# Narrow matmul passes of a decode-and-prefill kernel: gate columns joined to wide units, the compressed branch issued between them, and scores for head pairs

## The chip, the cores and the metric

One core of one Trainium2 chip runs the whole program in one launch. The metric is the device time of that launch in microseconds, lower is better; the shown time is a median of three runs.

## The reference

Two layers are computed for 512 prompt tokens and for 8 sequences of 8 new tokens each (D = 1024, all in 32-bit floats). Layer A is a matrix-memory layer with a pooled branch; layer C is sparse attention with three branches: compressed keys and values, selected pages, and a sliding window. What the change touches is the projection of layer C and the prompt's compressed branch:

```python
q, kc_raw, vc_raw, ks, vs, kw, vw, gate_logits(48), z = split(rmsnorm(x) * mod @ c_w_in)
gates   = sigmoid(gate_logits + b_gate)                  # 16 heads x 3 branches
pooled  = sum over blocks of 32 tokens (stride 16) of pos * raw        # 31 blocks for the prompt
kc, vc  = gelu(pooled @ w1 + b1) @ w2                    # keys get a rotary position
out     = gates[0]*attend(q, kc, vc) + gates[1]*selected + gates[2]*window
y       = x + gate * ((out * silu(z)) @ c_w_out)
```

## The kernel before

The program is a row of blocks, each with a stream of its own for TensorE (PE), VectorE (DVE), ScalarE (ACT), GpSimd (POOL) and SyncE (SP), tied by semaphores. All engines meet in a barrier between two blocks. The order of work within a stream is written out by hand.

The **projection of layer C** is `project(pe, "c", plan_c, ...)`. `plan_c` is a list of units, and a unit is one output tile: kind "T" (token-major, at most 128 tokens x 512 columns; the 128x128 activations are the stationary weights, the weight matrix moves), kind "F" (feature-major, 128 features x 576 tokens in two halves of 288), kind "N" (narrow). Before, they were: units 0 to 4 "T" for the raw compressed keys and values (`W_CC`), 5 to 8 "F", 9 to 13 "T", 14 to 21 "F" for the queries, 22 to 29 "F" for z, and 30 to 34 "N", the 48 gate columns for five tiles of tokens. Each unit sums over KT = 8 slices of D. Units rotate over three pairs of PSUM banks (0 to 5), ACT copies each out (L1229 for T, L1236 and L1237 for F, L1231 for N), and PE starts unit u only after unit u-3 was copied. Banks 6 and 7 are for the rotary position: one unit behind each key or query unit, `swap` issues two matmuls (L1209, L1210), and DVE does four operations (L1283 to L1289). Tiles 0 to 3 of a "T" or "N" group have 128 prompt tokens each, tile 4 the samples' 64.

After the projection, DVE adds the gate bias (L1300) and ACT takes the sigmoid (L1240). A **second block** computes the prompt's compressed branch: pooling matmuls (L1350), the gate rows of the samples (L1354), the hidden layer (L1310, then ACT L1314), the keys in two forms (L1318, L1319), the values (L1364), and DVE's part of it, which ends with the gate rows (L1391, L1394). A **third block** is the attention. It begins with `prompt_cmp_scores` for both halves of the heads (L1528), which DVE masks (L1633) and takes a maximum of (L1639), while PE goes on to `pe_pool` (L1679, L1686). SP and POOL send the cached pages from this block's start (L1520).

A 32-bit matmul shows in the trace as two passes, each a LDWEIGHTS and a MATMUL record, so that a unit of 8 matmuls is 16 passes.

Of the kernel before, what the change touches and what calls it, by code (L numbers as in the profile page):

```python
# [17 lines left out]
P = 128  # L18
# [3 lines left out]
NB = 8  # L22
# [231 lines left out]
def build(nc, v):  # L254

    with ExitStack() as ctx:
# [48 lines left out]
        plan_c += [(W_ZC + n // 4, "F", n) for n in range(8)] + [(None, "N", n) for n in range(5)]  # L305
# [26 lines left out]
        def project(pe, name, plan, moving, narrow, between=None, ready=None, each_step=None, halves_apart=None):  # L332
# [16 lines left out]
            for i, (chunk, kind, index) in enumerate(plan):  # L349
# [39 lines left out]
                elif kind == "T":  # L389
                    m = P if index < 4 else NS  # L390
                    for k in range(KT):
                        last = pe.matmul(main[0:m, :], moving[k][:, index * P:index * P + m], w[:, k, :],  # L392
                                         start=(k == 0), stop=(k == KT - 1))
                        if k == 2:
                            add_parts()
                elif name == "a":
                    for k in range(KT):
                        pe.matmul(main[0:H, :], narrow[:, k, H * index:H * index + H], moving[k][:, 0:TP],
                                  start=(k == 0), stop=(k == KT - 1))
                        if k == 2:  # L400
                            add_parts()
                    for k in range(KT):
                        last = pe.matmul(samp[0:H, 0:NS], narrow[:, k, H * index:H * index + H], moving[k][:, TP:NT],
                                         start=(k == 0), stop=(k == KT - 1))
                else:
                    m = P if index < 4 else NS
                    for k in range(KT):
                        last = pe.matmul(main[0:m, 0:48], moving[k][:, index * P:index * P + m], narrow[:, k, 8:56],
                                         start=(k == 0), stop=(k == KT - 1))
# [657 lines left out]
        kcP = take(2 * NC_P).rearrange("p (c n) -> p c n", c=2)  # L1067
# [93 lines left out]

        in_d, swapped, roped, set_up = sem("in_d"), sem("swapped"), sem("roped"), sem("set_up")
# [5 lines left out]
        with nc.Block() as block:  # L1168
            @block.sync
            def _(sp):  # L1170
                sp.dma_start(constD, v["constD"]).then_inc(in_d, 16)
                sp.dma_start(constC, v["constC"]).then_inc(in_d, 16)
                sp.dma_start(ktmp_[:, 0:320], v["pool_masks"]).then_inc(in_d, 16)
                sp.dma_start(narrow_, v["narrow"]).then_inc(in_d, 16)
# [12 lines left out]
            def _(pool):  # L1187
                pool.memset(gates_, 0.0)
                pool.memset(qblk, 0.0)
                pool.memset(w1b, 0.0)  # L1190
# [3 lines left out]
            def _(pe):  # L1194
                def ready(i):
                    if i < 4:
                        pe.wait_ge(nC.h_prompt, i + 1)
                    if i == 4:
                        pe.wait_ge(nC.h_sample, 1)
                    if i == 5:  # L1200
                        pe.wait_ge(in_d, 64)
# [10 lines left out]
                project(pe, "c", plan_c, [hC[:, k, :] for k in range(KT)], narrow, between=swap, ready=lambda i, _: ready(i))  # L1212

            @block.scalar
            def _(act):
# [7 lines left out]
                for i, (chunk, kind, index) in enumerate(plan_c):  # L1223
# [6 lines left out]
                    elif chunk is None:  # L1230
                        last = act.activation(gates[0:m, index, :], main[0:m, 0:48], ACT.Copy)  # L1231
# [7 lines left out]
                act.wait_ge(gate_sum, 1)  # L1239
                act.activation(gates_, gates_, ACT.Sigmoid).then_inc(gate_sig, 1)  # L1240

            @block.vector
            def _(dve):
# [17 lines left out]
                dve.wait_ge(in_d, 64)  # L1261
# [12 lines left out]
                for g in range(2):  # L1274
                    rows, o = slice(g * DH, g * DH + DH), g * DH
                    dve.tensor_copy(w2b[rows, 2, o:o + 8], sm("w2k")[rows, 8:16])
                    dve.tensor_copy(w2b[rows, 2, o + 8:o + 16], sm("w2k")[rows, 0:8])
                for n in range(12):
# [20 lines left out]
                dve.wait_ge(proj_evac, u0c + len(plan_c))  # L1299
                dve.tensor_tensor(gates, gates, sm("b_gate").unsqueeze(1).to_broadcast([P, 5, 48]), ALU.add).then_inc(gate_sum, 1)  # L1300
# [4 lines left out]

        def compress_dve_pool(dve, n):
            return dve.tensor_tensor(pooled[:, :, 0:n], lohi[:, :, 0, 0:n], lohi[:, :, 1, 1:n + 1], ALU.add)
# [21 lines left out]

        def compress_dve_keys(dve, kcT, n, bank, bank2):  # L1330
            cos = cd("cmp_cos")[:, 0:n].unsqueeze(1).to_broadcast([P, 2, n])
            sin = cd("cmp_sin")[:, 0:n].unsqueeze(1).to_broadcast([P, 2, n])
            a = ps[:, bank, 0:2 * n].rearrange("p (c n) -> p c n", c=2)
            b = ps[:, bank2, 0:2 * n].rearrange("p (c n) -> p c n", c=2)
            dve.tensor_tensor(kcT[:, :, 0:n], a, cos, ALU.mult)
            dve.tensor_tensor(ktmp[:, :, 0:n], b, sin, ALU.mult)
            dve.drain()
            return dve.tensor_tensor(kcT[:, :, 0:n], kcT[:, :, 0:n], ktmp[:, :, 0:n], ALU.add)

        pe_p, act_p, dve_p = sem("pe_pcmp"), sem("act_pcmp"), sem("dve_pcmp")  # L1340
        PE2 = Order(["pool", "gates", "hidk", "hidv", "kc", "vc"])
        AC2 = Order(["hk", "hv", "vcs"])
        DV2 = Order(["lohi", "pooled", "kcT", "gates"])
        with nc.Block() as block:
            @block.tensor
            def _(pe):
                for c in range(4):
                    for t in range(4):
                        out = ps[:, 0, c * P:(c + 1) * P].rearrange("p (l n) -> p l n", l=2)[:, :, t * 8:t * 8 + 8]
                        last = pe.matmul(out, ccz[:, t, c * P:c * P + P], wpos[:, c // 2], start=True, stop=True)  # L1350
                last.then_inc(pe_p, PE2.one("pool"))
                rt = cc_("row_token", NS).rearrange("p (b n) -> p b n", b=NB)
                for b in range(NB):
                    last = pe.matmul(ps[:, 2, b * 48:b * 48 + 48], rt[:, b, :], gates[0:NS, 4, :], start=True, stop=True)  # L1354
                last.then_inc(pe_p, PE2.one("gates"))
                pe.wait_ge(dve_p, DV2["pooled"])
                compress_pe_hidden(pe, 0, NC_P, 1).then_inc(pe_p, PE2.one("hidk"))
                compress_pe_hidden(pe, 1, NC_P, 7).then_inc(pe_p, PE2.one("hidv"))
                pe.wait_ge(act_p, AC2["hv"])
                compress_pe_keys(pe, NC_P, 3, 4).then_inc(pe_p, PE2.one("kc"))  # L1360
                for gp in range(2):
                    for g2 in range(2):
                        rows = slice(g2 * DH, g2 * DH + DH)
                        last = pe.matmul(ps[g2 * NC_P:g2 * NC_P + NC_P, 5, gp * DH:gp * DH + DH], hid[rows, 2 + gp, 0:NC_P],  # L1364
                                         sm("w2v")[rows, :], start=True, stop=True)
                last.then_inc(pe_p, PE2.one("vc"))

            @block.scalar
            def _(act):
                act.wait_ge(pe_p, PE2["hidk"])  # L1370
                compress_act_hidden(act, 0, NC_P, 1).then_inc(act_p, AC2.one("hk"))
                act.wait_ge(pe_p, PE2["hidv"])
                compress_act_hidden(act, 1, NC_P, 7).then_inc(act_p, AC2.one("hv"))
                act.wait_ge(pe_p, PE2["vc"])
                act.activation(vcP, ps[0:2 * NC_P, 5, 0:P], ACT.Copy).then_inc(act_p, AC2.one("vcs"))

            @block.vector
            def _(dve):
                dve.memset(lohi[:, :, 1, NC_P:NC_P + 1], 0.0)
                dve.wait_ge(pe_p, PE2["pool"])  # L1380
                dve.tensor_copy(lohi[:, :, :, 0:32], ps[:, 0, :].rearrange("p (c l n) -> p c l n", c=4, l=2)[:, :, :, 0:32])\
                    .then_inc(dve_p, DV2.one("lohi"))
                dve.drain()
                compress_dve_pool(dve, NC_P).then_inc(dve_p, DV2.one("pooled"))
                dve.wait_ge(pe_p, PE2["kc"])
                compress_dve_keys(dve, kcP, NC_P, 3, 4).then_inc(dve_p, DV2.one("kcT"))
                dve.wait_ge(pe_p, PE2["gates"])
                dve.drain()
                g3_ = ktmp.rearrange("p c n -> p (c n)")[:, 0:NB * 48]
                g3 = g3_.rearrange("p (b c) -> p b c", b=NB)  # L1390
                dve.tensor_tensor(g3, ps[:, 2, 0:NB * 48].rearrange("p (b c) -> p b c", b=NB),  # L1391
                                  cc_("row_head").unsqueeze(1).to_broadcast([P, NB, 48]), ALU.mult)
                dve.drain()
                dve.tensor_reduce(grow, g3_.rearrange("p (b h c) -> p b c h", b=NB, c=3), AX.X, ALU.add)\  # L1394
                    .then_inc(dve_p, DV2.one("gates"))

# [126 lines left out]
        def prompt_cmp_scores(pe, gp):  # L1523
            for r in range(R):
                for t in range(4):
                    for g2 in range(2):
# [914 lines left out]
```

## Time and profile before

| | |
|---|---|
| median of three runs | 1384.14 us (1380.78 to 1392.83) |
| the profiled execution | 1385.89 us, span 1384.2 us |
| mean granted TensorE clock | 0.930 |
| PE busy | 1244.8 us, 90% |
| PEld (weight loads) busy | 782.9 us, 57% |
| DVE, ACT, POOL busy | 485.4, 412.9, 175.3 us |

The units 0 to 34 of the projection stand from 511.26 to 764.5 us, the second block from 766.7 to 782.2 us, and the attention from 782.3 us to the end. "idle before <- releaser" behind a row says how long the engine had been idle and who ended it. A granted clock of 1.00 is 2.4 GHz and 0.50 is 1.2 GHz.

### The profile page before, as it was taken

The page shows a single profiled execution, that of the slowest core. Times are in us where ns is not written, and L with a number is a line of the kernel's source. Part 1 is how long each engine was busy: PE and PEld are TensorE (multiplying, and loading weights), DVE is VectorE, ACT ScalarE, POOL GpSimd, SP SyncE. Part 2 cuts the span into 40 slices and gives each one's busy share as a digit, 9 for nine tenths or more (in the row PEclk, how much of TensorE's full clock was granted, in tenths as well). Part 3 has the DMA queues.
Part 4 walks back from the last instruction along what each step waited for, and adds up shares of the span by engine and source line. Part 5 has one row for each costly group of instructions (what it writes and reads, how often), then busy time and mean ns, then how long its engine had stood idle before and what let it go on. Part 6 is the DMA issues. An engine that isn't in the chain of part 4 may idle for free. (4 is left out here: it accounts for less than half of the span.)

```text
span 1384.2 us, 25565 instructions
## 1 busy us (share of the span) xinstructions
PE 1244.8 (90%) x9287; PEld 782.9 (57%) x9287; DVE 485.4 (35%) x1478; ACT 412.9 (30%) x1088; POOL 175.3 (13%) x287
## 2 busy tenths in 40 slices
PE   4899999992986979999999889999999799989996
PEld 1676755751654744747778845555555434444455
DVE  2352120004564240101210175556555433333334
ACT  3311111112220031000101146565556433333443
POOL 0000000001000000000000122222222353343300
PEclk8999999995786989999999589999999999999998
DMA  9414333338003131212300377666666698999972
GB/s 388 171 61 182 122 122 122 122 133 280 24 10 121 61 135 36 74 38 75 125 0 1 110 262 241 223 224 230 224 229 222 231 342 296 329 318 318 339 268 70
DMA packets 94905, 238.01 MB, mean 172 GB/s; under 512 B 11450, under 2 KB 49468, under 8 KB 90300
## 3 DMA queue, kind: packets, MB, share of 16 engines
q1 hardware_dynamic: 74076, 169.26, 35.0%
q0 software_dynamic: 20704, 67.13, 13.5%
q8 instruction: 74, 1.21, 0.4%
q14 instruction: 51, 0.42, 0.1%
HBM read 227.68 MB, written 17.05 MB: 177 GB/s over the span
## 5 line engine op out<-in xcount | busy, mean ns | idle before, releaser
L385 PE MATMUL ps<-arena,wring 128*128 128x288 f32 x1664 | 416.9, 412 | 6.9 <-DMA wring<-in_weights 5.4
L385 PEld LDWEIGHTS ps<-arena,wring 128*128 128x128 f32 x1664 | 318.2, 192 | 100.0 <-issue 8.0
L1520 POOL DMA_DIRECT2D arena<-in_cmp_pages x128 | 70.1, 549 | 489.5 <-issue 278.7
L392 PE MATMUL ps<-wring,arena 128*128 128x512 f32 (+1 forms) x240 | 107.8, 608 | 7.1 <-ACT arena L1220 7.1
L1614 DVE CUSTOM_DVE_ANT_0 wring<-ps,wring 128x128 f32<-128x128 f32 (+3 forms) x128 | 57.6, 488 | 75.8 <-PE ps L1543 74.1
L392 PEld LDWEIGHTS ps<-wring,arena 128*128 128x128 f32 (+1 forms) x240 | 43.4, 184 | 67.5 <-issue 60.3
L1606 ACT ACTIVATE wring<-ps 128x128 f32<-128x128 f32 (+3 forms) x128 | 49.0, 436 | 90.8 <-PE ps L1566 90.8
L2079 DVE CUSTOM_DVE_ANT_1 arena<-ps,small 128x512 f32<-128x512 f32 x64 | 44.3, 693 | 89.7 <-PE ps L1998 89.6
L2055 ACT ACTIVATE arena<-arena 128x512 f32<-128x512 f32 (+1 forms) x88 | 57.0, 649 | 60.1 <-DVE arena L2095 60.1
L1592 ACT ACTIVATE wring<-wring 128x128 f32<-128x128 f32 (+3 forms) x128 | 70.7, 559 | 8.4 <-DVE wring L1614 8.3
L1679 PE MATMUL ps<-arena 128*32 128x256 f32 x1024 | 70.1, 391 | 0.0
L2066 ACT ACTIVATE arena<-ps 128x512 f32<-128x512 f32 x72 | 43.0, 597 | 84.9 <-PE ps L2019 84.9
L1283 DVE SCALAR_TENSOR_TENSOR arena<-ps,arena 128x512 f32<-128x512 f32 x12 | 8.3, 693 | 151.7 <-PE ps L1210 151.7
L2141 PE MATMUL ps<-arena 128*128 128x512 f32 x128 | 60.8, 630 | 0.0
L1543 PE MATMUL ps<-arena 64*128 64x512 f32 (+3 forms) x256 | 52.9, 490 | 5.4 <-DVE wring L1614 5.4
L1962 POOL DMA_DIRECT2D wring<-in_kv_pages x64 | 45.2, 711 | 80.6 <-PE ps L2033 39.2
L1236 ACT ACTIVATE arena<-ps 128x288 f32<-128x288 f32 x20 | 8.2, 412 | 151.6 <-PE ps L385 151.6
L2019 PEld LDWEIGHTS ps<-fixed,arena 128*128 128x128 f32 x288 | 30.8, 140 | 39.4 <-ACT arena L2055 24.4
L1998 PE MATMUL ps<-wring,arena 128*64 128x512 f32 x144 | 39.5, 629 | 10.6 <-DMA wring<-in_win_kv 7.1
L1583 PE MATMUL ps<-wring,arena 128*64 128x128 f32 x640 | 48.7, 282 | 0.0
L1566 PE MATMUL ps<-fixed,wring 128*128 128x128 f32 x320 | 47.8, 280 | 1.1 <-ACT wring L1606 1.1
L1998 PE MATMUL ps<-arena 128*64 128x512 f32 x144 | 41.1, 655 | 7.7 <-DMA arena<-in_win_kv 7.4
(383 smaller groups left out, 1572.7 us busy)
## 6 DMA issues: line engine op xcount, KB each, us to landing
wring<-in_weights SPq DMA_DIRECT2D x27, 2048.0 KB, 9.0
arena<-in_cmp_pages SPq DMA_DIRECT2D x128, 256.0 KB, 3.5
arena<-in_cmp_pages POOLq DMA_DIRECT2D x128, 256.0 KB, 4.3
wring<-in_kv_pages SPq DMA_DIRECT2D x64, 256.0 KB, 9.3
wring<-in_kv_pages POOLq DMA_DIRECT2D x64, 256.0 KB, 6.8
arena<-in_kv_pages SPq DMA_DIRECT2D x50, 256.0 KB, 6.5
arena<-in_kv_pages POOLq DMA_DIRECT2D x50, 256.0 KB, 6.9
arena<-in_out_tiles SPq DMA_DIRECT2D x12, 512.0 KB, 8.4
```

The source lines that it names most:

```text
L385: last = pe.matmul(out[:, 0:HT], w[:, k, ct * P:ct * P + P], moving[k][:, half * HT:half * HT + HT], start=(k == 0), stop=(k == KT - 1))
L392: last = pe.matmul(main[0:m, :], moving[k][:, index * P:index * P + m], w[:, k, :], start=(k == 0), stop=(k == KT - 1))
L1520: eng.dma_start(cring[q % CR][:, 2 * half + j, :], v["cmp_pages"][bass.ds(ids[2 * d + j], 1)] .rearrange("o p c -> (o p) c")).then_inc(c_i ...
L1543: last = pe.matmul(ps[:, SB + g2, 0:(t + 1) * P], qT[rows, u, t * P:t * P + P], kk[rows, 2 * br + u // 4, 0:(t + 1) * P], start=True, stop ...
L1583: last = pe.matmul(ps[g2 * DH:g2 * DH + DH, OB, t * P:t * P + P], vv[:, n, o:o + DH], PTb[:, tile_no[i] % 3, g2, n * P:n * P + P], start=F ...
L1592: act.activation(Pb[:, b, h, 0:s], Pb[:, b, h, 0:s], ACT.Exp, scale=-1.0, bias=negm[:, b, h:h + 1], accum_out=sums[:, b, h:h + 1]).then_in ...
L1606: act.activation(PTb[:, tile_no[i] % 3, h, 0:s], ps[:, TB + h, 0:s], ACT.Copy).then_inc(act_a, AC3.one(("e", i, h)))
L1614: dve.tensor_tensor_reduce(Pb[:, b, h, 0:(t + 1) * P], ps[:, SB + h, 0:(t + 1) * P], causal4[:, (3 - t) * P:TP], -1.0, 3.0e38, ALU.add, AL ...
L1679: last = pe.matmul(ps[32 * j:32 * j + 32, half, x * KVW:x * KVW + KVW], wpool[:, x, 32 * q:32 * q + 32], page[:, j, x * KVW:x * KVW + KVW] ...
L1998: last = pe.matmul(out, qblk[:, gp, n, gp * DH:gp * DH + DH], keys, start=True, stop=True)
L2055: last = act.activation(SS[:, o:o + w], SS[:, o:o + w], ACT.Exp, scale=sign, bias=negmax[:, which:which + 1], accum_out=sums11[:, n % 2, c ...
L2141: last = pe.matmul(ps[:, 0, :], tile_w[:, k, :], zT[:, k, 0:TP], start=(k == 0), stop=(k == KT - 1))
```

## The change

1. The five "N" units of layer C go. Each of the units 0 to 4 gets, behind each of its 8 wide matmuls, a narrow one with the same stationary activations and the 48 gate columns, into the pair's other bank. ACT copies 48 more columns in each of these units. The narrow weights are sent first by SP, under a semaphore of their own, and DVE adds the gate bias ahead of the rotary work; ACT takes the sigmoid after unit 13.
2. The second block goes. Its matmuls are issued by `prompt_compressed` after the units 23 (`AT_POOL`: pooling and gate rows), 25 (`AT_HIDDEN`) and 27 (`AT_KEYS`: keys and values), in banks 6 and 7. ACT's gelu stands behind the copies of unit 25, its copy of the values behind unit 29. DVE's part stands behind the rotary work and `qblk`.
3. The compressed keys `kcP` become block diagonal over the two heads of a pair, with zeros from a POOL memset, so that one matmul with 128 contraction rows and 64 moving columns gives the scores of both heads, where before two matmuls with 64 rows and 32 columns each did. DVE's mask is four operations a half, of 256 elements a row, where it was two of 512.

```diff
-        plan_c += [(W_ZC + n // 4, "F", n) for n in range(8)] + [(None, "N", n) for n in range(5)]
+        plan_c += [(W_ZC + n // 4, "F", n) for n in range(8)]
...
                         last = pe.matmul(main[0:m, :], moving[k][:, index * P:index * P + m], w[:, k, :],
                                          start=(k == 0), stop=(k == KT - 1))
+                        if chunk == W_CC:
+                            last = pe.matmul(samp[0:m, 0:48], moving[k][:, index * P:index * P + m], narrow[:, k, 8:56],
+                                             start=(k == 0), stop=(k == KT - 1))
...
-        kcP = take(2 * NC_P).rearrange("p (c n) -> p c n", c=2)
+        kcP = take(4 * NC_P).rearrange("p (c n) -> p c n", c=2)
...
+        AT_POOL, AT_HIDDEN, AT_KEYS = 23, 25, 27
...
+                sp.dma_start(narrow_, v["narrow"]).then_inc(in_narrow, 16)
                 sp.dma_start(constD, v["constD"]).then_inc(in_d, 16)
...
+                def prompt_compressed(i):
+                    if i == AT_POOL:
+                        pe.wait_ge(roped, 12)
+                        for c in range(4):
+                            for t in range(4):
+                                out = ps[:, 6, c * P:(c + 1) * P].rearrange("p (l n) -> p l n", l=2)[:, :, t * 8:t * 8 + 8]
+                                last = pe.matmul(out, ccz[:, t, c * P:c * P + P], wpos[:, c // 2], start=True, stop=True)
+                        last.then_inc(pe_p, PE2.one("pool"))
+                        pe.wait_ge(gate_sig, 1)
+                        rt = cc_("row_token", NS).rearrange("p (b n) -> p b n", b=NB)
+                        for b in range(NB):
+                            last = pe.matmul(ps[:, 7, b * 48:b * 48 + 48], rt[:, b, :], gates[0:NS, 4, :], start=True, stop=True)
+                        last.then_inc(pe_p, PE2.one("gates"))
+                    if i == AT_HIDDEN:
+                        pe.wait_ge(dve_p, DV2["pooled"])
...
+                    if i == AT_KEYS:
+                        pe.wait_ge(act_p, AC2["hv"])
+                        pe.wait_ge(dve_p, DV2["gates"])
...
+                def after_unit(i):
+                    swap(i)
+                    prompt_compressed(i)
...
-                    for g2 in range(2):
-                        rows, o = slice(g2 * DH, g2 * DH + DH), (r * 4 + t) * NC_P
-                        last = pe.matmul(ps[:, SB + 2 * gp + g2, o:o + NC_P], qT[rows, gp * 4 + r, t * P:t * P + P],
-                                         kcP[rows, gp, 0:NC_P], start=True, stop=True)
+                    o = (r % 2 * 4 + t) * 2 * NC_P
+                    last = pe.matmul(ps[:, SB + 2 * gp + r // 2, o:o + 2 * NC_P], qT[:, gp * 4 + r, t * P:t * P + P], kcP[:, gp, :],
+                                     start=True, stop=True)
```

On PE, at the start of layer C's projection (units 0 to 4, then unit 5 and 6), stood before:

```order
L392 MATMUL ps<-wring,arena 128x512 x32
L392 MATMUL ps<-wring,arena 64x512 x8
L385 MATMUL ps<-arena,wring 128x288 x32
L1209 MATMUL ps<-arena 128x512
L1210 MATMUL ps<-arena 128x64
```

Now the same place reads as follows, where "..." stands for 31 more such pairs, and after it for 7 more:

```order
L392 MATMUL ps<-wring,arena 128x512
L395 MATMUL ps<-arena 128x48
...
L392 MATMUL ps<-wring,arena 64x512
L395 MATMUL ps<-arena 64x48
...
L385 MATMUL ps<-arena,wring 128x288 x32
L1221 MATMUL ps<-arena 128x512
L1222 MATMUL ps<-arena 128x64
```

Behind each of the 40 wide matmuls, which stood in a row, there is now a narrow one.

On PE, from the last rotary swap (behind unit 22) to the first scores and `pe_pool`, stood before (L1168 and L1344 are the ends of the first and the second block):

```order
L1209 MATMUL ps<-arena 128x512
L1210 MATMUL ps<-arena 128x64
L385 MATMUL ps<-arena,wring 128x288 x112
L408 MATMUL ps<-arena 128x48 x32
L408 MATMUL ps<-arena 64x48 x8
L1168 UNCONDITIONAL_BRANCH
L1345 UNCONDITIONAL_BRANCH
L1350 MATMUL ps<-arena 128x2x8 x16
L1354 MATMUL ps<-arena 128x48 x8
...
L1528 MATMUL ps<-arena 128x32 x64
```

Now there stands (L1177 is the end of the only block left there):

```order
L385 MATMUL ps<-arena,wring 128x288 x16
L1230 MATMUL ps<-arena 128x2x8 x16
L1235 MATMUL ps<-arena 128x48 x8
L385 MATMUL ps<-arena,wring 128x288 x32
L1240 MATMUL ps<-arena 128x64 x2
L385 MATMUL ps<-arena,wring 128x288 x32
L1246 MATMUL ps<-arena 128x64 x2
L1252 MATMUL ps<-small,arena 32x64 x4
L385 MATMUL ps<-arena,wring 128x288 x32
L1177 UNCONDITIONAL_BRANCH
L2210 UNCONDITIONAL_BRANCH
L1532 MATMUL ps<-arena 128x64 x32
```

The row of 112 wide matmuls (units 23 to 29) is cut in four, the narrow groups stand in the cuts, and the scores are 32 matmuls where they were 64.

## Rows read from the trace of the kernel before

**Rows 1.** Waits, 510 to 800 us: who waited for whom, total, times, longest.
```profile
DVE arena L1283 <- PE ps L1210: 151.7, 12, 45.0
```

**Rows 2.** Timeline of PE at the end of the projection: start us, us, instructions.
```profile
752.33 12.18 PE L408 MATMUL ps<-arena 128*128 128x48 f32 x80
766.77 6.98 PE L1350 MATMUL ps<-arena 128*128 128x16 f32 x32 [2.27 <-PEq L1168]
773.68 3.65 PE L1354 MATMUL ps<-arena 64*128 64x48 f32 x16
777.26 1.11 PE L1310 MATMUL ps<-arena 128*128 128x64 f32 x4
...
779.82 0.64 PE L1364 MATMUL ps<-small,arena 64*32 64x64 f32 x8
782.30 13.86 PE L1528 MATMUL ps<-arena 64*128 64x32 f32 x128 [1.84 <-PEq L1344]
796.09 1.93 PE L1679 MATMUL ps<-arena 128*32 128x256 f32 x16
```

**Rows 3.** Stretches: us, busy time by engine, PEclk, DMA share, GB/s.
```profile
516.00:520.00 4.00, 4.00 (x9) 1.65 (x9) 3.79 (x16) 4.00 (x11) 0.00 (x0) 0.86 0.00 0
752.00:756.00 4.00, 4.00 (x37) 3.89 (x35) 0.00 (x0) 0.93 (x3) 0.00 (x0) 1.00 0.02 4
756.00:760.00 4.00, 4.00 (x21) 4.00 (x20) 0.00 (x0) 0.42 (x2) 0.00 (x0) 0.51 0.00 0
...
790.00:796.00 6.00, 6.00 (x58) 6.00 (x58) 0.74 (x2) 0.00 (x0) 0.79 (x2) 0.50 1.03 386
796.00:800.00 4.00, 4.00 (x32) 1.73 (x33) 3.56 (x5) 0.00 (x0) 0.00 (x0) 0.50 0.49 179
```

**Rows 4.** Timeline of ACT at the end of the projection.
```profile
752.83 0.41 ACT L1237 ACTIVATE arena<-ps 128x288 f32<-128x288 f32 x1
754.24 0.21 ACT L1231 ACTIVATE arena<-ps 128x48 f32<-128x48 f32 x1 [1.00 <-PE ps L408]
756.03 0.21 ACT L1231 ACTIVATE arena<-ps 128x48 f32<-128x48 f32 x1 [1.57 <-PE ps L408]
759.26 0.21 ACT L1231 ACTIVATE arena<-ps 128x48 f32<-128x48 f32 x1 [3.01 <-PE ps L408]
762.67 0.21 ACT L1231 ACTIVATE arena<-ps 128x48 f32<-128x48 f32 x1 [3.20 <-PE ps L408]
764.54 0.20 ACT L1231 ACTIVATE arena<-ps 64x48 f32<-64x48 f32 x1 [1.66 <-PE ps L408]
...
766.06 0.41 ACT L1240 ACTIVATE arena<-arena 128x240 f32<-128x240 f32 x1
...
780.51 0.27 ACT L1375 ACTIVATE arena<-ps 64x128 f32<-64x128 f32 x1 [1.78 <-PE ps L1364]
```

**Rows 5.** Timeline of PE around the last rotary swap.
```profile
688.90 8.00 PE L385 MATMUL ps<-arena,wring 128*128 128x288 f32 x32
...
697.60 0.33 PE L1210 MATMUL ps<-arena 128*128 128x64 f32 x2
697.77 54.72 PE L385 MATMUL ps<-arena,wring 128*128 128x288 f32 x224
```

**Rows 6.** Timelines of PE and of ACT at the start of the projection.
```profile
511.26 37.65 PE L392 MATMUL ps<-wring,arena 128*128 128x512 f32 x80 [7.07 <-ACT arena L1220]
...
528.20 0.60 ACT L1229 ACTIVATE arena<-ps 128x512 f32<-128x512 f32 x1 [6.20 <-PE ps L392]
535.07 0.60 ACT L1229 ACTIVATE arena<-ps 128x512 f32<-128x512 f32 x1 [6.27 <-PE ps L392]
```

**Rows 7.** Timeline of DVE: its last copies, the gate rows, a half's mask.
```profile
700.66 2.16 DVE L1297 COPY arena<-arena 64x64 f32<-64x64 f32 x16
...
781.31 0.67 DVE L1394 TENSOR_REDUCE arena<-arena 128x24 f32<-128x384 f32 x1
...
796.20 1.29 DVE L1633 TENSOR_TENSOR wring<-ps,wring 128x512 f32<-128x512 f32 x2 [5.46 <-PE ps L1528]
```

More of the change, by code:

```diff
@@ L403, in project @@
                         last = pe.matmul(samp[0:H, 0:NS], narrow[:, k, H * index:H * index + H], moving[k][:, TP:NT],
[L404 to L408, printed above, removed]
                                          start=(k == 0), stop=(k == KT - 1))
@@ L1197, in ready @@
                         pe.wait_ge(nC.h_prompt, i + 1)
+                    if i == 0:
+                        pe.wait_ge(in_narrow, 16)
                     if i == 4:
@@ L1210, in swap @@
                         pe.matmul(ps[:, 7, 0:NS], cc_("swap"), rope_tile[n][:, TP:NT], start=True, stop=True).then_inc(swapped, 1)
-                project(pe, "c", plan_c, [hC[:, k, :] for k in range(KT)], narrow, between=swap, ready=lambda i, _: ready(i))
+                def prompt_compressed(i):
[13 more added lines that the diff above has]
+                        pe.wait_ge(dve_p, DV2["pooled"])
+                        for x, name in enumerate(("hidk", "hidv")):
+                            pe.matmul(ps[:, 6, 2 * x * NC_P:2 * x * NC_P + 2 * NC_P].rearrange("p (c n) -> p c n", c=2), w1b[:, x, :],
+                                      pooledP[:, 2 * x:2 * x + 2], start=True, stop=True).then_inc(pe_p, PE2.one(name))
+                    if i == AT_KEYS:
+                        pe.wait_ge(act_p, AC2["hv"])
+                        pe.wait_ge(dve_p, DV2["gates"])
+                        for x, weights in enumerate((w2b[:, 0, :], w2b[:, 2, :])):
+                            last = pe.matmul(ps[:, 7, 2 * x * NC_P:2 * x * NC_P + 2 * NC_P].rearrange("p (c n) -> p c n", c=2), weights,
+                                             hidP[:, 0:2], start=True, stop=True)
+                        last.then_inc(pe_p, PE2.one("kc"))
+                        for g2 in range(2):
+                            rows, outs_ = slice(g2 * DH, g2 * DH + DH), slice(g2 * NC_P, g2 * NC_P + NC_P)
+                            for gp in range(2):
+                                last = pe.matmul(ps[outs_, 6, gp * DH:gp * DH + DH], hidP[rows, 2 + gp], sm("w2v")[rows, :],
+                                                 start=True, stop=True)
+                        last.then_inc(pe_p, PE2.one("vc"))
@@ L1214, in _ @@
+                def after_unit(i):
+                    swap(i)
+                    prompt_compressed(i)
+                project(pe, "c", plan_c, [hC[:, k, :] for k in range(KT)], narrow, between=after_unit, ready=lambda i, _: ready(i))
             @block.scalar
@@ L1229, in _ @@
                         last = act.activation(out[0:m, :], main[0:m, :], ACT.Copy)
-                    elif chunk is None:
-                        last = act.activation(gates[0:m, index, :], main[0:m, 0:48], ACT.Copy)
+                        if chunk == W_CC:
+                            last = act.activation(gates[0:m, index, :], samp[0:m, 0:48], ACT.Copy)
                     else:
@@ L1238, in _ @@
                     last.then_inc(proj_evac, 1)
-                act.wait_ge(gate_sum, 1)
-                act.activation(gates_, gates_, ACT.Sigmoid).then_inc(gate_sig, 1)
+                    if i == 13:
+                        act.wait_ge(gate_sum, 1)
+                        act.activation(gates_, gates_, ACT.Sigmoid).then_inc(gate_sig, 1)
+                    if i == AT_HIDDEN:
+                        for x, name in enumerate(("hk", "hv")):
+                            act.wait_ge(pe_p, PE2["hidv"])
+                            act.activation(hidP[:, 2 * x:2 * x + 2], ps[:, 6, 2 * x * NC_P:2 * x * NC_P + 2 * NC_P].rearrange("p (c n) -> p c n", c=2),
+                                           ACT.Gelu_apprx_tanh, bias=sm("b1kv"[:2] + "kv"[x])[:, 0:1]).then_inc(act_p, AC2.one(name))
+                act.wait_ge(pe_p, PE2["vc"])
+                act.activation(vcP, ps[0:2 * NC_P, 6, 0:P], ACT.Copy).then_inc(act_p, AC2.one("vcs"))
             @block.vector
@@ L1277, in _ @@
                     dve.tensor_copy(w2b[rows, 2, o + 8:o + 16], sm("w2k")[rows, 0:8])
+                dve.wait_ge(proj_evac, u0c + 5)
+                dve.tensor_tensor(gates, gates, sm("b_gate").unsqueeze(1).to_broadcast([P, 5, 48]), ALU.add).then_inc(gate_sum, 1)
                 for n in range(12):
@@ L1298, in _ @@
                                             qT[rows, gp * 4 + r, TP:NT].rearrange("p (b t) -> p b t", b=NB))
[L1299 to L1307, printed above, removed]
+                dve.wait_ge(pe_p, PE2["pool"])
+                dve.memset(lohiP[:, :, 1, NC_P:NC_P + 1], 0.0)
+                dve.tensor_copy(lohiP[:, :, :, 0:NC_P], ps[:, 6, :].rearrange("p (c l n) -> p c l n", c=4, l=2)[:, :, :, 0:NC_P])\
+                    .then_inc(dve_p, DV2.one("lohi"))
+                dve.drain()
+                dve.tensor_tensor(pooledP, lohiP[:, :, 0, 0:NC_P], lohiP[:, :, 1, 1:NC_P + 1], ALU.add).then_inc(dve_p, DV2.one("pooled"))
+                dve.wait_ge(pe_p, PE2["gates"])
+                g3 = gates3_.rearrange("p (b c) -> p b c", b=NB)
+                dve.tensor_tensor(g3, ps[:, 7, 0:NB * 48].rearrange("p (b c) -> p b c", b=NB),
+                                  cc_("row_head").unsqueeze(1).to_broadcast([P, NB, 48]), ALU.mult)
+                dve.drain()
+                dve.tensor_reduce(grow, gates3_.rearrange("p (b h c) -> p b c h", b=NB, c=3), AX.X, ALU.add)\
+                    .then_inc(dve_p, DV2.one("gates"))
+                dve.wait_ge(pe_p, PE2["kc"])
+                cos = cd("cmp_cos")[:, 0:NC_P].unsqueeze(1).to_broadcast([P, 2, NC_P])
+                sin = cd("cmp_sin")[:, 0:NC_P].unsqueeze(1).to_broadcast([P, 2, NC_P])
+                dve.drain()
+                dve.tensor_tensor(ktmpP[:, 0:2], ps[:, 7, 0:2 * NC_P].rearrange("p (c n) -> p c n", c=2), cos, ALU.mult)
+                dve.tensor_tensor(ktmpP[:, 2:4], ps[:, 7, 2 * NC_P:4 * NC_P].rearrange("p (c n) -> p c n", c=2), sin, ALU.mult)
+                dve.drain()
+                for g2 in range(2):
+                    rows = slice(g2 * DH, g2 * DH + DH)
+                    last = dve.tensor_tensor(kcP[rows, :, g2 * NC_P:g2 * NC_P + NC_P], ktmpP[rows, 0:2], ktmpP[rows, 2:4], ALU.add)
+                last.then_inc(dve_p, DV2.one("kcT"))
         def compress_pe_hidden(pe, x, n, bank):
@@ L1340, in build @@
[L1340 to L1361, printed above, removed]
-                    for g2 in range(2):
[L1363 to L1395, printed above, removed]
@@ L1630, in prompt_cmp_mask @@
             dve.wait_ge(pe_a, PE3["sc%d" % gp])
-            add = pcmp_add.rearrange("p (t n) -> p t n", t=4).unsqueeze(1).to_broadcast([P, R, 4, NC_P])
-            for g2 in range(2):
-                last = dve.tensor_tensor(pc[:, gp, g2::2, :].rearrange("p (r t) n -> p r t n", r=R),
-                                         ps[:, SB + 2 * gp + g2, :].rearrange("p (r t n) -> p r t n", r=R, t=4), add, ALU.add)
+            add = pcmp_add.rearrange("p (t n) -> p t n", t=4).unsqueeze(2).to_broadcast([P, 4, 2, NC_P])
+            for r in range(R):
+                got = ps[:, SB + 2 * gp + r // 2, r % 2 * 256:r % 2 * 256 + 256].rearrange("p (t g n) -> p t g n", t=4, g=2)
+                last = dve.tensor_tensor(pc[:, gp, 8 * r:8 * r + 8].rearrange("p (t g) n -> p t g n", t=4), got, add, ALU.add)
             last.then_inc(dve_a, DV3.one("ca%d" % gp))
```

29 lines of the change are left out of this document (15 added, 14 removed).

## The prediction

> **What bounds the kernel now.** I read the waits first: from 510 to 800 us the long ones are of DVE and ACT for PE, such as DVE's 151.7 us for the rotary matmuls [rows 1]; PE itself waits where a block ends. So in the projection the end is set by PE's own passes, and whatever is added to PE there is paid in full. Then I read PE's timeline from the last wide pass on [rows 2]: at 752.33 us the wide work is over, and `pe_pool` begins at 796.09 us. These 43.76 us are narrow units (12.18), the first barrier with the sigmoid (2.27), pooling (6.98), gate rows (3.65), hidden layer, keys and values (to 780.5), the end of DVE's part and the second barrier (PE idle 1.84), and scores (13.86). The third view is the granted clock [rows 3]: 1.00 from 752 to 756 us, 0.51 in the next four, 0.50 up to 800. Nearly all of the tail runs at 1.2 GHz.
>
> **What a narrow pass costs.** ACT's copies stand one narrow unit of 16 passes apart [rows 4]: 756.03 - 754.24 = 1.79 us, 112 ns a pass, at the upper level; 762.67 - 759.26 = 3.41 us, 213 ns, at the lower; 764.54 - 762.67 = 1.87 us, 117 ns, at the lower with 64 weight columns. Pooling moves 16 columns, not 48, and also takes 6.98/32 = 218 ns, so that the weights set this price and not the moving columns. Is it hidden between wide passes? A unit with a swap behind it takes 697.77 - 688.90 = 8.87 us, one without (752.33 - 697.77)/7 = 7.79 [rows 5]; the swap costs 1.08. Its two wide passes are worth 2 x 429 ns, by the copies of wide units at 528.20 and 535.07 [rows 6]. That leaves 0.22 us for its two narrow passes, 111 ns each: not hidden.
>
> **Part 1, gate columns in units 0 to 4.** Removed: 12.18 us at the end. Added: 80 narrow passes. PE starts at 511.26 us [rows 6] and the granted clock of 516 to 520 us is 0.86 [rows 3], so the upper level begins at about 517.1: 5.9 us are at the lower one. There a slice of D takes 2 x 857 + 2 x 213 ns = 2.14 us, 2.7 slices in all, 1.15 us added; the other 29.3 slices add 224 ns each, 6.56 us; the 8 of tile 4 add 16 passes of half of 117 ns, 0.94 us. Sum 8.65 us. Bounds: from above 11.6 us, if the level comes back 5.9 us later than before (half of that lost, 2.95); from below 3.1, if only the 48 columns' own time showed (48/512 of 429 ns, 40 ns a pass). PE waits for nothing within these 37.65 us, so no idle time takes the passes in. The narrow transfer goes ahead of three others by one issue, and their first user is at unit 5 or DVE behind the norm: nothing; the 5 extra copies of 0.21 us lie in ACT's idle 6.2 us a unit. DVE's bias now waits for unit 4, with the rotary work queued behind it, whose first swap comes two units later: nothing.
>
> **Part 2, the second block cut up.** Removed: everything from the first barrier to 782.30 us except one barrier. Added between wide units at the upper level: pooling and gate rows 48 x 112 ns = 5.4 us, hidden layer and keys 8 x 112 ns = 0.9, values half of 0.64 = 0.3; 6.6 us. But the level will not stay. Wide work ended at 752.33 and the level had fallen by about 756 [rows 3]: 3.7 us of narrow passes were enough. The group after unit 23 lasts 5.4 us, so I expect a fall inside it: its last 1.7 us are doubled (+1.7), and wide work that follows loses half of the time until the level returns, at most as long as at the stage's start (5.9 us, +2.9). I take +3.6 in all, 10.2 us. From below it is 6.6 (no fall), from above 6.6 + 1.7 + 2.9 = 11.2. The waits: `roped` 12 and the copies of `qblk` end by 702.8 [rows 7], the group's place is 697.77 + 7.79 = 705.6 us; `pooled`, ACT's gelu with two table loads, and DVE's key chain each have one or two units of 7.79 us. Behind PE's waits stand only its wide units, and none should be held.
>
> **The one barrier left.** ACT's last copy starts at 752.83 and takes 0.41, the copy of the values 0.27 [rows 4]: 753.5. From DVE's last end, 781.31 + 0.67, to the first score pass at 782.30 [rows 2, 7] are 0.32 us. So scores begin 1.5 us behind the last wide pass.
>
> **Part 3, scores.** Before, 128 passes of 64 rows in 13.86 us, 108 ns each at the lower level: two of them share the time of one full pass of 213. Now 64 full passes. At the lower level 64 x 213 = 13.6 us, a gain of nothing by their number; at the upper 64 x 112 = 7.2. With a fall 3.7 us after the wide work, 2.2 us or 20 passes are fast and 44 are not: 2.2 + 9.4 = 11.6 us. DVE's second mask stands on the path behind them: 1.29 us before for two operations [rows 7]; four of half the size cost between that and 2.58, and nearer the first since the elements are the same: +0.25.
>
> The page "TensorE: Matmul & The Clock Gate" of the Trainium skill, section "The mechanism", says that weight loads overlap running matmuls only where the row groups differ. By that, two heads in two row groups already ran together, and a count of matmuls (half as many, so 6.9 us and 4.7 less than my 11.6) misleads; the trace's 108 against 213 ns agrees.
>
> **The sum.** 43.76 - 8.65 - 10.2 - 1.5 - 11.6 - 0.25 = 11.6 us saved. Against the profiled execution, 1385.89, that is 1374.3. That execution was 1.75 above the median of the runs; against the median of 1384.14 it is **1372.5 us**, 0.8% faster. Behind 797 us the same chain of DVE and ACT follows (mask, maximum, exponential), so the saving should pass through.
>
> **Rivals.**
> A, as forecast, 60%: 1368 to 1378, by the bounds of the level's falls.
> B, narrow passes keep the 112 ns pace, 18%. Scores move 64 columns where the units that lost the level moved 48, and PE comes to them straight from wide work. Then 4.4 us more: 1368.1; if the group after unit 23 keeps it too, another 3.6: 1364.5. Against it: the level fell within 3.7 us of narrow passes, and the scores of before, at 790 to 796 us, stayed at 0.50 with PE busy throughout [rows 3]. The same page, section "LDWEIGHTS (loading the stationary operand)", gives columns/1.2 ns, 107 ns for 128, without naming a level; by it B would be the rule, but rows 4 show 112 and 213 ns for the same load.
> C, the narrow passes hide behind wide ones, 4%: then part 1 costs 3.1 us, 5.5 less: 1367. The swap's 0.22 us speaks against it.
> D, the saving is taken back by the next thing that is late, 13%. Page transfers begin with the attention block, and the DMA engines are full from 790 to 796 us (1.03 of their time, 386 GB/s) [rows 3]. `pe_pool` will want its first pages 2.3 us sooner after the block's start; if they come no sooner, those 2.3 us are lost: 1374.8. If PE also waits at the three cuts, one to two us each: up to 1381.
> E, slower, 5%: the merged units never reach the upper level. Narrow-only work did not regain it in 40 us, and a merged unit is one fifth narrow. The 31.7 us of units 0 to 4 that ran behind 517.1 us would double, and the 6.56 + 0.94 us of narrow passes too: +39, so 1412. Each us later costs half of one, so it decides from 23 us later on, when the saving is gone. For it speaks only that the level needed 5.9 us of unbroken wide passes.
>
> **Chances.** 1% (13.8 us) is about what a measurement of this kernel tells from no change. The forecast is 2.2 us short of it. Faster by over 1%: B, C, and a quarter of A, 0.37. Slower: E, 0.05. Same: 0.58. Eight in ten: 1364 (both falls absent) to 1380 (D with waits).
>
> **What the changed profile should show.** Units 0 to 4 in 46.3 us instead of 37.65; a granted clock of 0.50 for some us behind unit 23; 12 to 15 us between the last wide pass and `pe_pool`, with scores of 10 to 13 us, beginning at the upper level; no narrow unit at the end and one barrier fewer. Units 0 to 4 below 43 us would prove part 1 wrong, scores in 7.2 us part 3, and idle time of PE at the cuts part 2. The total goes wrong most easily by the level: each fall costs 1.5 to 3 us, and where one lies can differ between executions.

## The result

The changed kernel took 1373.37 us (median of 12 runs, 1366.6 to 1384.56), the kernel before in the same sessions 1388.43 us. The ratio is 0.9903, with a 95% interval of 0.9874 to 0.9932: 13.5 us faster, with 9.4 to 17.5 as the interval. The profiled execution took 1367.46 us, with a span of 1365.7 us and a mean clock of 0.948.

The timeline of PE in the changed kernel, from the first group between wide units to `pe_pool` (start us, us, instructions), answers to [rows 2] and [rows 5]:

```profile
715.86 3.64 PE L1230 MATMUL ps<-arena 128*128 128x16 f32 x32
719.42 2.43 PE L1235 MATMUL ps<-arena 64*128 64x48 f32 x16
721.78 18.70 PE L385 MATMUL ps<-arena,wring 128*128 128x288 f32 x64
740.32 0.55 PE L1240 MATMUL ps<-arena 128*128 128x64 f32 x4
740.71 15.79 PE L385 MATMUL ps<-arena,wring 128*128 128x288 f32 x64
756.33 0.55 PE L1246 MATMUL ps<-arena 128*128 128x64 f32 x4
756.82 0.42 PE L1252 MATMUL ps<-small,arena 64*32 64x64 f32 x8
757.17 15.84 PE L385 MATMUL ps<-arena,wring 128*128 128x288 f32 x64
774.21 7.33 PE L1532 MATMUL ps<-arena 128*128 128x64 f32 x64 [1.21 <-PEq L1177]
784.08 1.94 PE L1683 MATMUL ps<-arena 128*32 128x256 f32 x16 [2.54 <-DMA arena<-in_cmp_pages]
```

Read it by differences of starts. The first group takes 721.78 - 715.86 = 5.92 us, the two wide units behind it take 18.54, where the next two take 15.62 (740.71 to 756.33): 2.92 us are lost there. The hidden layer adds 0.39 us, keys and values 0.84. The scores take 7.33 us; before they took 13.86. And there is a wait that was not there before: PE idles 2.54 us ahead of `pe_pool`, for a page.

The stretches of the changed kernel (us, busy time by engine, PEclk, DMA share, GB/s), as in [rows 3]:

```profile
513.50:519.40 5.90, 5.88 (x10) 3.04 (x11) 5.60 (x7) 5.06 (x14) 0.00 (x0) 0.50 0.33 135
519.40:550.00 30.60, 30.60 (x116) 17.08 (x114) 3.43 (x21) 6.36 (x18) 0.00 (x0) 1.00 0.00 1
716.00:720.00 4.00, 4.00 (x38) 3.97 (x37) 0.42 (x2) 0.71 (x2) 0.00 (x0) 1.00 0.01 4
720.80:727.60 6.80, 6.80 (x18) 5.09 (x18) 1.23 (x2) 0.00 (x0) 0.00 (x0) 0.50 0.00 0
727.60:740.00 12.40, 12.40 (x52) 9.62 (x51) 0.00 (x0) 0.71 (x2) 0.00 (x0) 1.00 0.00 0
773.00:782.00 9.00, 7.33 (x65) 7.22 (x64) 1.84 (x6) 2.15 (x4) 3.78 (x7) 1.00 0.54 175
782.30:789.00 6.70, 4.92 (x32) 1.87 (x32) 5.11 (x10) 1.06 (x1) 0.98 (x3) 0.50 1.03 388
```

The clock fell inside the group behind unit 23, 4.9 us after its first pass, and came back 6.8 us later; a fall was forecast there. It did not fall in the scores: the sixth row says 1.00, where [rows 3] had 0.50 for the same work. It fell only behind them, while PE waited.

The start of the projection in the changed kernel, timeline of PE, as in [rows 6]:

```profile
513.52 2.08 PE L392 MATMUL ps<-wring,arena 128*128 128x512 f32 x2 [7.07 <-ACT arena L1268]
...
519.69 1.09 PE L392 MATMUL ps<-wring,arena 128*128 128x512 f32 x2
520.62 0.32 PE L395 MATMUL ps<-arena 128*128 128x48 f32 x2
520.77 1.09 PE L392 MATMUL ps<-wring,arena 128*128 128x512 f32 x2
...
551.15 1.07 PE L392 MATMUL ps<-wring,arena 128*64 128x512 f32 x2
552.06 0.27 PE L395 MATMUL ps<-arena 128*64 128x48 f32 x2
552.16 1.04 PE L392 MATMUL ps<-wring,arena 128*64 128x512 f32 x2
...
559.08 15.84 PE L385 MATMUL ps<-arena,wring 128*128 128x288 f32 x64
```

Units 0 to 4 take 559.08 - 513.52 = 45.56 us, where they took 37.6. A slice of D at the upper level lasts 520.77 - 519.69 = 1.08 us instead of 2 x 0.429: the two narrow passes cost 0.22 us.

ACT at the end of the projection and DVE behind the scores, as in [rows 4] and [rows 7]:

```profile
773.35 0.41 ACT L1285 ACTIVATE arena<-ps 128x288 f32<-128x288 f32 x1
773.64 0.27 ACT L1296 ACTIVATE arena<-ps 64x128 f32<-64x128 f32 x1
```

```profile
781.58 1.42 DVE L1638 TENSOR_TENSOR wring<-ps,wring 128x256 f32<-128x256 f32 x4 [2.08 <-PE ps L1532]
783.08 1.22 DVE L1643 TENSOR_REDUCE wring<-wring 128x32 f32<-128x1024 f32 x1
...
790.59 0.68 DVE L1618 CUSTOM_DVE_ANT_0 wring<-ps,wring 128x512 f32<-128x512 f32 x1
```

The last row is the first maximum of a prompt tile. It serves below as the end of the **stage**: from PE's first matmul of the projection to this operation, 790.59 - 513.52 = 277.1 us. Before, the same operation began at 805.07 us (timeline of DVE in the kernel before):

```profile
805.07 0.69 DVE L1614 CUSTOM_DVE_ANT_0 wring<-ps,wring 128x512 f32<-128x512 f32 x1
```

The stage was then 805.07 - 511.26 = 293.8 us. So the change took 16.7 us out of the stage of this execution.

### The profile page after: what moved, and what is told of

It is laid out like the page before. It is cut to its first block and busy times, and to the rows that moved or that the text cites. A ratio compares the mean times of both kernels' runs of the same rounds, so it can differ in the third digit from the quotient of the medians.

```text
span 1365.7 us, 25435 instructions
## 1 busy us (share of the span) xinstructions
PE 1226.4 (90%) x9223; PEld 769.5 (56%) x9223; DVE 485.8 (36%) x1483; ACT 413.7 (30%) x1089; POOL 175.9 (13%) x288
## 5 line engine op out<-in xcount | busy, mean ns | idle before, releaser
L392 PE MATMUL ps<-wring,arena 128*128 128x512 f32 (+1 forms) x240 | 115.4, 616 | 7.1 <-ACT arena L1268 7.1
L392 PEld LDWEIGHTS ps<-wring,arena 128*128 128x128 f32 (+1 forms) x240 | 40.1, 183 | 46.0 <-issue 38.8
L1683 PEld LDWEIGHTS ps<-arena 128*32 128x32 f32 x1024 | 26.9, 110 | 38.2 <-issue 22.6
```

The source lines that it names most:

```text
L1683: last = pe.matmul(ps[32 * j:32 * j + 32, half, x * KVW:x * KVW + KVW], wpool[:, x, 32 * q:32 * q + 32], page[:, j, x * KVW:x * KVW + KVW] ...
```

## The experiments

Each kernel was timed beside the kernel before. The stage is read from its profiled execution in the same manner.

| kernel | stage, us | ratio to before (95%) |
|---|---|---|
| before | 293.8 | 1 |
| changed | 277.1 | 0.9903 (0.9874 to 0.9932) |
| changed, once more | 277.1 | 0.9901 (0.9872 to 0.9929) |
| part 1 alone | 287.3 | 0.9974 (0.9956 to 0.9992) |
| part 3 alone | 294.2 | 1.0008 (0.9987 to 1.0029) |
| changed, part 3 undone | 282.4 | 0.9920 (0.9889 to 0.9950) |
| changed, scores of 32 columns | 296.1 | 1.0004 (0.9977 to 1.0031) |
| changed, narrow units behind unit 4 | 280.6 | 0.9906 (0.9870 to 0.9942) |
| changed, groups cut | 273.8 | 0.9842 (0.9805 to 0.9880) |
| groups cut, mask later | 270.5 | 0.9819 (0.9788 to 0.9851) |

**The changed kernel once more.**

> The changed kernel once more, beside the others on the same chip: 0.99 of the time before, with scores of 7.3 us at the upper level and a fall of the level behind unit 23, if both are properties of the program and not of one execution.

The ratio and the stage repeat to 0.0002 and 0.1 us, and so does the level in the scores (timeline of PE and stretch):

```profile
775.57 7.33 PE L1532 MATMUL ps<-arena 128*128 128x64 f32 x64 [1.21 <-PEq L1177]
```

```profile
775.50:783.00 7.50, 7.33 (x64) 7.22 (x64) 1.49 (x5) 1.28 (x1) 3.41 (x7) 1.00 0.71 203
```

The fall behind unit 23 came 4.9 us into the group here too. The whole span, though, was 1377.5 us against 1365.7. The start of the first output tile tells where the difference lies (timeline of PE, the changed kernel, then the second execution of it):

```profile
1102.81 3.70 PE L2145 MATMUL ps<-arena 128*128 128x512 f32 x8
```

```profile
1105.20 7.13 PE L2145 MATMUL ps<-arena 128*128 128x512 f32 x16
```

From there to the end one execution took 262.9 us and the other 272.3. The part at the end varies by 9 us with the code unchanged, while the stage varies by hardly 0.1. That is why the total has an interval of 8 us, and why a few microseconds are judged by the stage.

**Part 1 alone.** The kernel before with this, and with the bias and the sigmoid early:

```diff
-        plan_c += [(W_ZC + n // 4, "F", n) for n in range(8)] + [(None, "N", n) for n in range(5)]
+        plan_c += [(W_ZC + n // 4, "F", n) for n in range(8)]
...
+                        if chunk == W_CC:
+                            last = pe.matmul(samp[0:m, 0:48], moving[k][:, index * P:index * P + m], narrow[:, k, 8:56],
+                                             start=(k == 0), stop=(k == KT - 1))
```

> Part 1 alone: the kernel before with the gate columns in units 0 to 4, and the bias and the sigmoid early. Own theory: 12.2 us of narrow units go and 8.0 us come back in units 0 to 4; beyond that the second block now follows wide work, so its pooling runs at the upper level (3.6 us for 7.0) and the barrier has no sigmoid in front of it (about 1 us less). Sum: 8 to 9 us faster than before, 0.6%. Rival: the merged passes only move the cost, and the second block is as slow as before: 4 us faster.

It saved 6.5 us of the stage, and 0.26% in all, where 8 to 9 us and 0.6% were expected. The narrow units gave 4.2 us, as expected. The rest fell short (timeline of PE):

```profile
761.65 5.69 PE L1352 MATMUL ps<-arena 128*128 128x16 f32 x32 [1.06 <-PEq L1167]
767.27 3.65 PE L1356 MATMUL ps<-arena 64*128 64x48 f32 x16
```

The barrier cost 1.2 us less, and the pooling 5.69 instead of 6.98 us, not 3.6. The clock fell at 763 us, 1.4 us into the pooling (stretches):

```profile
758.00:763.00 5.00, 3.94 (x24) 3.08 (x22) 0.06 (x1) 2.00 (x3) 0.00 (x0) 1.00 0.00 0
763.00:775.00 12.00, 10.65 (x54) 9.97 (x53) 1.96 (x7) 0.90 (x3) 0.00 (x0) 0.50 0.00 0
```

**Part 3 alone.** The kernel before with block-diagonal keys:

```diff
-                    for g2 in range(2):
-                        rows, o = slice(g2 * DH, g2 * DH + DH), (r * 4 + t) * NC_P
-                        last = pe.matmul(ps[:, SB + 2 * gp + g2, o:o + NC_P], qT[rows, gp * 4 + r, t * P:t * P + P],
-                                         kcP[rows, gp, 0:NC_P], start=True, stop=True)
+                    o = (r % 2 * 4 + t) * 2 * NC_P
+                    last = pe.matmul(ps[:, SB + 2 * gp + r // 2, o:o + 2 * NC_P], qT[:, gp * 4 + r, t * P:t * P + P], kcP[:, gp, :],
+                                     start=True, stop=True)
```

> Part 3 alone: the kernel before with block-diagonal keys and one matmul for two heads. Own theory: the stage is at the lower level, 64 full passes of 213 ns take 13.7 us where 128 half passes took 13.86, and the time is the same as before within 1 us. Rival: half as many passes take half the time, 6.9 us faster.

```profile
784.50 13.89 PE L1533 MATMUL ps<-arena 128*128 128x64 f32 x64 [2.06 <-PEq L1350]
```

64 full passes take 13.89 us at the lower level, 217 ns each; the 128 half ones took 13.86 [rows 2]. Half the count gains nothing. The stage is 0.4 us longer.

**Part 3 undone in the changed kernel.** 

```diff
-                    o = (r % 2 * 4 + t) * 2 * NC_P
+                    for g2 in range(2):
+                        rows, o = slice(g2 * DH, g2 * DH + DH), (r * 4 + t) * NC_P
...
-                    last = dve.tensor_tensor(kcP[rows, :, g2 * NC_P:g2 * NC_P + NC_P], ktmpP[rows, 0:2], ktmpP[rows, 2:4], ALU.add)
+                    last = dve.tensor_tensor(kcP[rows, :, 0:NC_P], ktmpP[rows, 0:2], ktmpP[rows, 2:4], ALU.add)
```

> The changed kernel with part 3 undone: two matmuls of 64 rows and 32 columns for each pair again. Theory A: the level holds because PE comes to the scores from wide work after little more than a microsecond; then the 128 passes take 54 ns each, 6.9 us, and the time is that of the changed kernel within 1 us. Theory B: it holds because full passes of 64 columns keep the array busy enough; then half-filled passes let it fall after some 2 us, the scores take 10 to 13 us, and the kernel is 3 to 5 us slower than the changed one.

The timeline of PE, then the stretches:

```profile
772.51 12.80 PE L1533 MATMUL ps<-arena 64*128 64x32 f32 x128 [1.21 <-PEq L1177]
```

```profile
771.00:773.70 2.70, 1.49 (x24) 1.22 (x22) 0.00 (x0) 2.09 (x4) 0.00 (x0) 1.00 0.12 14
773.70:784.00 10.30, 10.30 (x101) 10.30 (x100) 1.29 (x2) 0.05 (x1) 4.46 (x8) 0.50 0.85 284
```

The half passes came to the scores from the same wide work, after the same barrier, and the clock fell 1.2 us later. They took 12.80 us for 7.33, and the stage is 5.4 us longer: theory B. The total says the same with less force (0.9920 against 0.9903, intervals overlap).

**Scores of 32 columns in full passes.**

```diff
-                    o = (r % 2 * 4 + t) * 2 * NC_P
-                    last = pe.matmul(ps[:, SB + 2 * gp + r // 2, o:o + 2 * NC_P], qT[:, gp * 4 + r, t * P:t * P + P], kcP[:, gp, :],
-                                     start=True, stop=True)
+                    for g2 in range(2):
+                        o = ((r % 2 * 4 + t) * 2 + g2) * NC_P
+                        last = pe.matmul(ps[:, SB + 2 * gp + r // 2, o:o + NC_P], qT[:, gp * 4 + r, t * P:t * P + P],
+                                         kcP[:, gp, g2 * NC_P:g2 * NC_P + NC_P], start=True, stop=True)
```

> The changed kernel with each score matmul cut in two of 32 moving columns, all 128 rows kept: 128 full passes where there are 64. Theory A, the level held because PE comes to the scores from wide work: 128 x 112 ns = 14.3 us at the upper level, 7 us slower than the changed kernel. Theory B, it held because 64 columns in full passes keep the array busy enough, and half of them do not: the level falls within 2 to 4 us of the first score, the rest goes at 213 ns, and the scores take 22 to 25 us, 15 to 18 us slower than the changed kernel.

Timeline of PE and stretches:

```profile
774.27 26.40 PE L1533 MATMUL ps<-arena 128*128 128x32 f32 x128 [1.21 <-PEq L1177]
```

```profile
772.00:775.40 3.40, 2.19 (x16) 1.66 (x14) 0.00 (x0) 2.03 (x4) 0.00 (x0) 1.00 0.04 10
775.40:800.00 24.60, 24.60 (x118) 24.60 (x118) 1.42 (x4) 0.12 (x1) 4.46 (x8) 0.50 0.52 184
```

Again the clock fell 1.2 us after the first score, and all gain of the change was gone (1.0004). Theory B, with a price 1.4 us beyond its range: 26.4 us, and a stage longer by 19.1. Theory A would have had 14.3 us.

**The narrow units early, not merged.**

```diff
-        plan_c = [(W_CC, "T", n) for n in range(5)] + [(W_KK, "F", n) for n in range(4)]
+        plan_c = [(W_CC, "T", n) for n in range(5)] + [(None, "N", n) for n in range(5)] + [(W_KK, "F", n) for n in range(4)]
```

> The changed kernel with part 1 replaced: the gate columns are five narrow units of their own again, but behind unit 4, not at the end. It tells the merging from the earlier place. Own theory: 74 passes' worth at the upper level is 8.0 us, as merged, but 80 narrow passes in a row make the level fall after 3.7 us; the rest takes twice as long and the wide work behind it loses up to 3 us: 4 to 7 us slower than the changed kernel. Rival: the narrow passes cost the same wherever they stand, and only the end of the stage mattered: same time as the changed kernel.

Timeline of PE and stretches:

```profile
551.75 10.48 PE L399 MATMUL ps<-arena 128*128 128x48 f32 x80
562.16 16.93 PE L385 MATMUL ps<-arena,wring 128*128 128x288 f32 x64
578.93 1.02 PE L1223 MATMUL ps<-arena 128*128 128x512 f32 x2
```

```profile
552.00:557.50 5.50, 5.50 (x52) 5.50 (x51) 0.00 (x0) 1.03 (x4) 0.00 (x0) 1.00 0.85 310
557.60:564.30 6.70, 6.70 (x35) 5.95 (x35) 0.41 (x1) 0.42 (x2) 0.00 (x0) 0.50 0.14 56
```

The clock fell 5.8 us into the narrow units and took 1.1 us from the wide work behind them: 11.5 us for the 8.0 of the merged passes, a stage 3.5 us longer. That is a little under the range given (whose 74 passes' worth are 72: 64 and half of 16). The total does not show it (0.9906): 3.5 us are within the noise of the end part. So about 3.5 us of part 1's worth in the changed kernel is the merging. The rest is the earlier place; how much that is here no run shows, since none leaves the narrow units at the end beside parts 2 and 3.

**The groups cut.**

```diff
-        AT_POOL, AT_HIDDEN, AT_KEYS = 23, 25, 27
+        AT_POOL, AT_GATES, AT_HIDDEN, AT_KEYS = 23, 25, 26, 28
...
-                        for c in range(4):
+                        for c in ((0, 1) if i == AT_POOL else (2, 3)):
```

> The changed kernel with the group behind unit 23 cut in three: half of the pooling behind unit 23, half behind 24, the gate rows behind 25, the hidden layer behind 26, keys and values behind 28, so that no narrow group is longer than 1.8 us. Own theory: the granted clock stays at 1.00 through the units 22 to 29, the 3.0 us lost behind unit 23 come back, and the kernel is about 3 us faster than the changed one, 17 to 18 faster than before. Rival: several short groups make the level fall once each, or the total of narrow passes is what counts: no gain or a loss of some us.

By this, half of the pooling stands behind unit 23 and half behind 24, the gate rows behind 25, and the two later groups one unit further on. Stretches from ahead of the first group to behind the hidden layer's passes, and over the scores:

```profile
715.00:746.00 31.00, 31.00 (x156) 25.12 (x155) 1.94 (x5) 3.52 (x9) 0.00 (x0) 1.00 0.00 1
770.50:778.00 7.50, 7.33 (x64) 7.21 (x64) 1.54 (x5) 1.26 (x1) 3.46 (x7) 1.00 0.65 211
```

The clock stays at 1.00 and the stage is 3.2 us shorter than the changed kernel's, where 3 was expected. The total is 0.9842; its interval just meets that of the changed kernel (0.9880 and 0.9874), so this step too is read from the stage.

**The second half's mask later**, on top of the groups cut:

```diff
-                prompt_cmp_mask(dve, 1)
                 prompt_cmp_max(dve, 0)
+                prompt_cmp_mask(dve, 1)
```

> The kernel with the groups cut (as in the run before) and, on DVE, the second half's mask behind the first half's maximum instead of ahead of it. Own theory: what is late behind the scores is the chain mask, maximum, subtraction, exponential, sum; with the maximum of the first half computed while PE does the second half's scores, the first maximum of a prompt tile (L1618 of the changed kernel) comes 3 to 3.5 us sooner, and the time falls by as much against the kernel with the groups cut. Rival: the pages for the pooling of the cached keys are late then (PE waited 2.5 us for them in the changed kernel, hidden by that chain), and at most 1 us is gained.

Timelines of DVE and of PE:

```profile
776.51 1.22 DVE L1646 TENSOR_REDUCE wring<-wring 128x32 f32<-128x1024 f32 x1
...
779.20 1.41 DVE L1641 TENSOR_TENSOR wring<-ps,wring 128x256 f32<-128x256 f32 x4
...
784.12 0.69 DVE L1621 CUSTOM_DVE_ANT_0 wring<-ps,wring 128x512 f32<-128x512 f32 x1
```

```profile
780.11 1.07 PE L1686 MATMUL ps<-arena 128*32 128x256 f32 x16 [1.65 <-DMA arena<-in_cmp_pages]
```

The maximum now runs under the second half's scores, and the stage is 3.4 us shorter again, 270.5 us. PE still waits 1.65 us for a page, and DVE's chain still hides it. This version is the fastest one, 0.9819; against the run before it the step is seen in the stage alone, since the intervals of the totals overlap.

## Why the prediction was right, and where not

The forecast of 1372.5 us and a saving of 11.6 us stands against 1373.37 us and 13.5 us by the ratio (9.4 to 17.5). The path was right; one term was mis-sized, and the total came out close in part by luck. The stage became 16.7 us shorter and not 11.6, and 4.3 of these 5.1 us are the scores. The total shows 13.5 of it, with an interval that holds both 11.6 and 16.7. The time itself is only 0.9 us off in part because the kernel before took 1388.43 us in these sessions, 4.3 more than the median from which the forecast started. The saving of 0.97% lies at the 1% at which the chances were divided, and its interval reaches to both sides of that.

| term | forecast | measured in the profile |
|---|---|---|
| units 0 to 4, added | 8.65 | 45.56 - 37.6 = 8.0 |
| groups between wide units, with the fall | 10.2 | 5.92 + 2.92 + 0.39 + 0.84 = 10.1 |
| last wide pass to first score | 1.5 | 1.4 |
| scores | 11.6 | 7.3 |
| second mask, added | 0.25 | 0.12 |

By the measured column 43.76 us lose 16.8, which is the stage's 16.7.

**Part 1.** The price of 112 ns for a narrow pass between wide ones held, and the clock rose 5.9 us after the start as before. The 0.65 us too many have a reason in the sum: I charged the narrow passes of the slow stretch at their lower pace, but that stretch lasts 5.9 us and loses half of them, without the narrow passes (before) and with them (after). 32 x 0.224 + 0.94 = 8.1 us would have been right. (The lower bound of 3.1 us is 3.2 by its own 80 x 40 ns; nothing hangs on it.) Rival E (the merged units never reach the upper level) did not occur: 1.00 from 519.4 us on.

**Part 2.** One fall was forecast and came, 6.8 us long, and its price was 3.4 us for the 3.6 forecast. Its two halves were not as forecast: the level fell 4.9 us into the group and not 3.7, so that the group itself lost 0.5 us (5.92 against 5.4) and not 1.7, and the wide work behind it lost 2.9, all of the bound. The cut groups show that it was the length of the group and not the narrow passes as such: with none longer than 2 us, none fell and 3.2 us came back. No wait at the cuts arose.

**Part 3, the step that was mis-sized.** I took the scores for narrow work like any other and let the clock fall 3.7 us behind the wide work. It never fell: 7.3 us where 11.6 were forecast, the first half of rival B and the prediction's own sign that part 3 was wrong. What was wrong is the reason: I took every pass that is priced by its weights for the same, since 16 and 48 moving columns cost the same time. For the clock 64 moving columns and 32 were not the same. Three kernels that came to the scores from the same wide work, 1.4 us later, separate it: 64 columns in 128 rows kept the level for all 7.3 us (in all five profiled executions with such scores behind wide work), 32 columns in 128 rows lost it after 1.2 us, and so did 32 columns in two halves of 64 rows. The time per pass did not change with the columns (26.4 us for 128 passes, mostly at 213 ns), the clock did. So part 3 is worth nothing by its count, as forecast and as part 3 alone shows, and 5.4 us by the clock, once parts 1 and 2 bring PE to it straight from wide work. The parts are not additive: part 1 alone gives 6.5 us of the stage and part 3 alone -0.4, both with part 2 16.7; parts 1 and 2 without part 3 give 11.4.

**The end.** Rival D was there in kind, and not in price: PE waited 2.5 us for the first pages, but the chain of mask, maximum, exponential and sum was later still: PE's first scores of a prompt tile ended at 789.46 us, 1.1 us ahead of the operation that ends the stage, and the stage lost nothing. As the groups cut and mask later show, that chain is the next thing to shorten.

**The excess.** The profiled pair differs by 18.4 us where the stage gave 16.7. The rest is 3.0 us less behind the first output tile and 1.0 less between the stage and it, with a stage that began 2.3 us later. Over the ten profiled executions the time behind that tile lies between 262.7 and 272.3 us, that between the stage and it between 312.1 and 314.3, in no order with the changes. Unprofiled executions of the changed kernel differ by up to 18 us; where these lie no trace shows, and which transfer or clock step varies was not tried.

**Open.** Whether rows count for the clock as columns do: the kernel with half the rows had half the columns too, and none had 64 columns in 64 rows. Whether the scores would keep the level after a longer idle time was not tried either, nor part 2 alone.

## What to carry to other kernels

Work of narrow passes is cheapest in short groups between wide work, since its price doubled wherever the clock fell (112 and 213 ns a pass), and a fall also costs the wide work behind it: groups under 2 us kept the clock here, one of 5.9 us lost 3 us more. Where two half-filled passes run side by side, joining them does not save their time, but fuller passes can keep the clock up, and that was the larger term here (5.4 us of the stage). Judge such a change by the length of the stage in the profile, and then look at what is late next; here it was a chain on another engine whose order could be changed for nothing.

## What the runs showed of the hardware that was not expected

A 32-bit pass with 128 weight columns in 128 rows took about 112 ns at the upper level and 213 to 217 ns at the lower, with 16, 32, 48 or 64 moving columns alike; with 64 weight columns about half (0.12 us for two passes in unit 4 of the changed kernel). Yet the granted clock told 64 columns from 32: at the same pace, the first stayed at 1.00 through 7.3 us and the second fell to 0.50 after 1.2 us. The fall did not always come after the same time: 3.7 us after the last wide pass before, 4.9 us in the group behind unit 23, 5.8 us in the narrow units put behind unit 4, and about 2.6 us, idle time of the barrier included, where a barrier followed the wide work: with part 1 alone, with part 3 undone, and with scores of 32 columns in full passes. Why these differ no run shows.
